# A router that counts instead of searching, four-byte token rows in 32 products, and an expert loop written out

## The reference, cut to what matters

```python
def moe_swiglu(h, router, w_in, w_out):
    b, s, d = h.shape
    t = h.reshape(b * s, d)
    logits = (t @ router).astype(jnp.float32)
    top_vals, top_idx = lax.top_k(logits, TOP_K)
    gates = jax.nn.softmax(top_vals, axis=-1)
    combine = jnp.sum(jax.nn.one_hot(top_idx, N_EXPERTS, dtype=jnp.float32) * gates[..., None], axis=1)
    y = jnp.zeros_like(t)
    for e in range(N_EXPERTS):
        y = y + combine[:, e:e + 1].astype(t.dtype) * swiglu(t, w_in[e], w_out[e])
    return y.reshape(b, s, d)
```

## Time and profile before

| | us |
|---|---|
| median of 3 runs (1569.7 to 1570.82) | 1569.99 |
| the profiled execution, its device time | 1570.96 |
| its span, first to last instruction | 1569.2 |
| around the span | 1.76 |
| PE busy | 1513.6 (96%) |
| DVE busy | 1199.7 (76%) |
| ACT busy | 994.5 (63%) |
| mean granted clock of PE | 0.986 |

### The profile page before, as it was taken

How to read it: one execution, slowest core, us unless ns; L and a number is a source line. 1 busy time by engine, 2 the same in 40 slices (tenths; PEclk the granted TensorE clock), 3 DMA queues, 4 the chain that set the end, 5 groups by cost and what they waited for, 6 DMA issues and landing times.

```text
span 1569.2 us, 21897 instructions
## 1 busy us (share of the span) xinstructions
PE 1513.6 (96%) x8223; PEld 1276.2 (81%) x8223; DVE 1199.7 (76%) x1033; ACT 994.5 (63%) x855; POOL 127.1 (8%) x192
## 2 busy tenths in 40 slices
PE   6999999999999699999999999999998999999998
PEld 6967999989997478888888877888887888888886
DVE  6966544565485768888888888888987888888887
ACT  5657433465545567776776676677776677677774
POOL 8900000000152300000000000000000000000000
PEclk9979999999999899999999999999999999999999
DMA  9503655546500369999999999999998999999994
GB/s 302 188 1 120 210 183 186 186 149 200 184 32 21 127 242 368 336 366 341 348 360 345 348 340 335 355 346 360 354 341 323 340 347 364 347 343 366 346 364 163
DMA packets 205346, 426.88 MB, mean 272 GB/s; under 512 B 6737, under 2 KB 56074, under 8 KB 205242
## 3 DMA queue, kind: packets, MB, share of 16 engines
q1 hardware_dynamic: 204880, 424.78, 76.6%
q0 software_dynamic: 320, 0.69, 0.2%
q10 hardware_dynamic: 42, 0.01, 0.0%
HBM read 424.41 MB, written 1.05 MB: 271 GB/s over the span
## 4 chain that ended last, share of the span: by engine, by line
PE 68%; DVE 2%; ACT 1%; issue 1%; DVEq 0%; ACTq 0%
PE bank L1287 20%; PE bank L1288 20%; PE bank L1289 20%; PE bank L1541 2%; PE bank L1647 2%; PE bank L1618 1%; DVE w_l L275 1%; PE bank L1523 0%; PE bank L1522 0%; PE bank L1631 0%; PE bank L1630 0%; ACT w_h L270 0%; PE bank L1554 0%; DVE h_l L511 0%; PE bank L1564 0%
## 5 line engine op out<-in xcount | busy, mean ns | idle before, releaser
L275 DVE TENSOR_TENSOR w_l<-raw,w_h 128x2048 fp32r<-128x2048 f32 x403 | 922.0, 2291 | 259.1 <-ACT w_h L270 258.1
L270 ACT ACTIVATE w_h<-raw 128x2048 fp32r<-128x2048 f32 x403 | 772.8, 1918 | 404.3 <-PE bank L1289 402.3
L1287 PE MATMUL bank<-w_h,hs_h 128*128 128x512 f32 x896 | 359.5, 401 | 6.5 <-issue 2.6
L1288 PE MATMUL bank<-w_l,hs_h 128*128 128x512 f32 x896 | 353.5, 395 | 3.7 <-issue 3.7
L1289 PE MATMUL bank<-w_h,hs_l 128*128 128x512 f32 x896 | 353.8, 395 | 0.0
L1287 PEld LDWEIGHTS bank<-w_h,hs_h 128*128 128x128 f32 x896 | 168.1, 188 | 45.2 <-issue 3.0
L1289 PEld LDWEIGHTS bank<-w_h,hs_l 128*128 128x128 f32 x896 | 168.0, 187 | 44.9 <-issue 4.1
L1287 PE MATMUL bank<-h_h,w_h 128*128 128x256 f32 x672 | 193.0, 287 | 6.3 <-DVE h_l L511 6.3
L1288 PEld LDWEIGHTS bank<-w_l,hs_h 128*128 128x128 f32 x896 | 168.3, 188 | 37.9
L1288 PE MATMUL bank<-h_l,w_h 128*128 128x256 f32 x672 | 191.1, 284 | 0.0
L1289 PE MATMUL bank<-h_h,w_l 128*128 128x256 f32 x672 | 191.0, 284 | 0.0
(11 more groups left out here) (275 smaller groups left out, 1413.0 us busy)
## 6 DMA issues: line engine op xcount, KB each, us to landing
raw<-in_moe_w_in SPq DMA_DIRECT2D x224, 1024.0 KB, 5.7
raw<-in_moe_w_out SPq DMA_DIRECT2D x112, 1024.0 KB, 5.5
raw<-in_ffn_w_in SPq DMA_DIRECT2D x22, 1024.0 KB, 5.1
raw<-in_hgrn_w_in SPq DMA_DIRECT2D x16, 1024.0 KB, 5.5
raw<-in_ffn_w_out SPq DMA_DIRECT2D x11, 1024.0 KB, 4.9
raw<-in_ab_w_in SPq DMA_DIRECT2D x10, 1024.0 KB, 11.7
raw<-in_ab_w_out SPq DMA_DIRECT2D x4, 1024.0 KB, 5.0
raw<-in_hgrn_w_out SPq DMA_DIRECT2D x4, 1024.0 KB, 4.9
```

Of the source, the lines that this page charges most:

```text
L270: act.activation(w_h[:, u0 % S, :], raw[:, u0 % R, :], ACT.Copy).then_inc(w_high, 1)
L275: eng.tensor_tensor(w_l[:, u0 % S, :], raw[:, u0 % R, :], w_h[:, u0 % S, :], ALU.subtract).then_inc(w_low, 1)
L1287: pe.matmul(o, a_high, b_high, start=start, stop=False, skip_group_check=True)
L1288: pe.matmul(o, a_high, b_low, start=False, stop=False, skip_group_check=True)
```

## The change

1. **Router by counting.** DVE compares each logit with the other seven of its token in one instruction of 128 elements (`above`, greater), once more with "greater or equal", takes the second where the other expert comes earlier (`earlier`), and adds up: a count of 0 is the first choice, of 1 the second, under 1.5 means chosen. The marks go to `chosen` in bf16 with zeros around, so that the ranks are two bf16 products and the expert totals a third. The gates (`gates`) are made after the first gather's results are out, and ACT's Exp moves behind `gather_high`. `slot_no` counts from 1, so that `rank` needs no -1.
2. **Token rows.** DVE makes `x_g` straight from `x` (`token_rows`, two instructions between those of the norm), ACT copies `x_h` (four bytes, F32R), DVE subtracts for `x_l` (`token_low`). POOL does none of it. A gather is 32 matmuls with `x_h`, `x_l` and a four-byte `sel`; `turn_selection` uses a four-byte identity.
3. **Order.** The lows of units `U_MOE + 1` and `U_MOE + 2` (`split_low`) move from ahead of the router to behind `choose` and behind `gather_low`.
4. **PE between.** Eight matmuls of 512 bf16 columns behind the turn of the logits, and three behind the ranks (`keep_warm`), whose results nothing reads.
5. **Experts.** In round 0 `moe_experts` writes all eight experts out, with no hardware loop.
6. **POOL's tables.** `span` and `lmask` share memory with layer 0's tensors, so POOL builds them after `o_part` 1, in the last unit of layer 0's attention output.

The diff, cut to these (the allocation, the semaphores' names and the round that isn't taken are left out):

```diff
+            if r == 0:
+                for e in range(NE):
+                    expert(e, e, 0, e % 2, e == NE - 1)
+                return
...
+            pool.wait_ge(o_part, 1)
             step(pool.memset(span[:].bitcast(F32), 1.0))
             step(pool.memset(lmask[:], 0))
...
-            for tt in range(TT):
-                pool.wait_ge(n_xn, 2 * (TT * 3 + tt) + 2)
-                pool.tensor_tensor(x_g[:, tt, :], xn[:, tt, :], gain_row[:], ALU.mult).then_inc(x_gain, 1)
-            for part in range(2):
-                for tt in range(TT):
-                    pool.wait_ge(x_part, 2 * part + tt + 1)
-                    dst = x_g[:, tt, :] if part == 0 else x_b[:, 2, tt, :]
-                    pool.tensor_tensor(dst, x_g[:, tt, :], x_b[:, part, tt, :], ALU.subtract).then_inc(x_gain, 1)
...
+            def token_rows(tt):
+
+                dve.wait_ge(gain_in, 16)
+                dve.scalar_tensor_tensor(out=x_g[:, tt, :], in0=x[:, tt, :], scalar=n_stat[:, 3, 4, tt:tt + 1], in1=gain_row[:],
+                                         op0=ALU.mult, op1=ALU.mult).then_inc(x_gain, 1)
+
+            def token_low(tt):
+
+                dve.wait_ge(x_high, tt + 1)
+                dve.tensor_tensor(x_l[:, tt, :], x_g[:, tt, :], x_h[:, tt, :], ALU.subtract).then_inc(x_low, 1)
...
             norm_low(3, C_FFN + 8)
-            split_low(dve, U_MOE + 1)
-            split_low(dve, U_MOE + 2)
+            token_low(0)
...
             dve.tensor_copy(logit_t[:], bank[0:NE, 4, 0:T]).then_inc(r_lc, 1)
+            token_low(1)
             dve.wait_ge(r_lg, 1)
             step(dve.tensor_copy(logit[:, 0, :, :], bank[:, 5, 0:TT * NE].rearrange("p (a e) -> p a e", a=TT)))
+            mine = logit[:, 0, :, :].unsqueeze(3).to_broadcast([P, TT, NE, NE])
+            other = logit[:, 0, :, :].unsqueeze(2).to_broadcast([P, TT, NE, NE])
+            dve.tensor_tensor(above[:, 0, :, :, :], other, mine, ALU.is_gt).then_inc(r_d, 1)
+            done[0] += 1
+            step(dve.tensor_tensor(above[:, 1, :, :, :], other, mine, ALU.is_ge))
+            step(dve.copy_predicated(above[:, 0, :, :, :], earlier[:], above[:, 1, :, :, :]))
+            step(dve.tensor_reduce(logit[:, 1, :, :], above[:, 0, :, :, :], AX.X, ALU.add))
+            dve.wait_ge(r_pad, 1)
+            step(dve.tensor_scalar(chosen[:, 1:3, 0:NE], logit[:, 1, :, :], 1.5, None, ALU.is_lt))
+            n_const["sel"] = done[0]
...
                 choose(0, r, 0)
                 if r == 0:
-                    step(dve.tensor_reduce(pick[:, 9, 0:1], bank[:, 4, TT * NE:(TT + 1) * NE], AX.X, ALU.max))
+                    split_low(dve, u + 1)
+                    dve.wait_ge(r_rank, 2)
...
                 gather_low(n0, 0)
+                if r == 0:
+                    split_low(dve, u + 2)
+                    gates()
...
+            for tt in range(TT):
+                act.wait_ge(x_gain, tt + 1)
+                act.activation(x_h[:, tt, :], x_g[:, tt, :], ACT.Copy).then_inc(x_high, 1)
+            act.wait_ge(const, n_const["early"])
+            act.activation(ident_r[:], ident[:], ACT.Copy).then_inc(id_r, 1)
             split_high(act, U_MOE + 2)
...
                 gather_high(n0, 0)
+                if r == 0:
+                    act.wait_ge(r_d, n_const["exp"])
+                    act.activation(pick[:, 5, :], pick[:, 4, :], ACT.Exp).then_inc(r_e, 1)
+                    table(ACT.Silu)
                 split_high(act, u + 3)
...
+            keep_warm(8, 7)
             pe.wait_ge(r_d, n_const["sel"])
-            s0, s1 = logit[:, 6, 0, :], logit[:, 6, 1, :]
-            pe.matmul(bank[:, 4, 0:NE], before[:], s0, start=True, stop=True)
-            pe.matmul(bank[:, 4, NE:2 * NE], ones[:], s0, start=True, stop=False)
-            pe.matmul(bank[:, 4, NE:2 * NE], before[:], s1, start=False, stop=True)
-            pe.matmul(bank[:, 4, 2 * NE:3 * NE], ones[:], s0, start=True, stop=False)
-            pe.matmul(bank[:, 4, 2 * NE:3 * NE], ones[:], s1, start=False, stop=True).then_inc(r_rank, 1)
+            pe.matmul(bank[:, 4, 0:P], before_b[:], chosen[:, 1:3, :], start=True, stop=False)
+            pe.matmul(bank[:, 4, 0:P], ones_b[:], chosen[:, 0:2, :], start=False, stop=True).then_inc(r_rank, 1)
+            pe.matmul(bank[:, 3, 0:P], ones_b[:], chosen[:, 1:3, :], start=True, stop=True).then_inc(r_rank, 1)
+            pe.wait_ge(id_r, 1)
+            keep_warm(3, 7)
...
-                            for part in range(3):
-                                last = pe.matmul(bank[:, 5 + i, c * P:(c + 1) * P], x_b[:, part, tt, f], sel[:, b, tt, :],
+                            for part, rows in enumerate((x_h, x_l)):
+                                last = pe.matmul(bank[:, 5 + i, c * P:(c + 1) * P], rows[:, tt, f], sel[:, b, tt, :],
...
-                    last = pe.matmul(bank[:, 7, tt * P:(tt + 1) * P], sel[:, b, tt, :], ident_h[:], start=True, stop=True)
+                    last = pe.matmul(bank[:, 7, tt * P:(tt + 1) * P], sel[:, b, tt, :], ident_r[:], start=True, stop=True)
```

More of the change, by code:

```diff
@@ L94, in build @@
         ident = sb("ident", [P, P])
-        ones = sb("ones", [P, P])
         mean_all = sb("mean_all", [P, P])
         mean_64 = sb("mean_64", [P, P])
-        before = sb("before", [P, P])
+        before_b = sb("before_b", [P, P], BF16)
+        ones_b = sb("ones_b", [P, P], BF16)
+        earlier = sb("earlier", [P, TT, NE, NE], I8)
+        ident_r = sb("ident_r", [P, P], F32R)
         slot_no = sb("slot_no", [P, 2, P])
@@ L308, in _ @@
                 pool.dma_start(router[:], A["moe_router"][0].rearrange("(c p) e -> p c e", p=P)).then_inc(rout_in, 16)
-            step(pool.memset(ones[:], 1.0))
+            step(pool.memset(ones_b[:], 1.0))
             step(pool.memset(mean_all[:], 1.0 / P))
@@ L830, in _ @@
-            step(dve.tensor_tensor(logit[:, 7, :, :], logit[:, 4, :, :], wide(pick[:, 7, :]), ALU.mult))
-            step(dve.tensor_tensor(logit[:, 8, :, :], logit[:, 5, :, :], wide(pick[:, 8, :]), ALU.mult))
-            step(dve.memset(comb[:], 0.0))
-            step(dve.memset(rank[:], -1.0))
-            step(dve.tensor_tensor(comb[:].rearrange("p (a e) -> p a e", a=TT)[:, :, 0:NE], logit[:, 7, :, :], logit[:, 8, :, :], ALU.add))
-            dve.wait_ge(r_rank, 1)
-            step(dve.scalar_tensor_tensor(out=logit[:, 9, :, :], in0=bank[:, 4, 0:TT * NE].rearrange("p (a e) -> p a e", a=TT), scalar=1.0,
-                                          in1=logit[:, 6, :, :], op0=ALU.add, op1=ALU.mult))
@@ L839, in _ @@
-            step(dve.tensor_scalar(rank[:].rearrange("p (a e) -> p a e", a=TT)[:, :, 0:NE], logit[:, 9, :, :], -1.0, None, ALU.add))
+            mine = logit[:, 0, :, :].unsqueeze(3).to_broadcast([P, TT, NE, NE])
[3 more added lines that the diff above has]
+            step(dve.tensor_tensor(above[:, 1, :, :, :], other, mine, ALU.is_ge))
@@ new lines, in _ @@
+            step(dve.tensor_reduce(pick[:, 0, :], logit[:, 0, :, :], AX.X, ALU.max))
+            step(dve.scalar_tensor_tensor(out=logit[:, 3, :, :], in0=logit[:, 4, :, :], scalar=-3.0e38, in1=logit[:, 0, :, :],
+                                          op0=ALU.mult, op1=ALU.add))
+            dve.wait_ge(r_rank, 1)
+            step(dve.scalar_tensor_tensor(out=rank[:].rearrange("p (a e) -> p a e", a=TT)[:, :, 0:NE],
+                                          in0=bank[:, 4, 0:P].rearrange("p (a e) -> p a e", a=TT)[:, :, 0:NE], scalar=1.0,
+                                          in1=chosen[:, 1:3, 0:NE], op0=ALU.add, op1=ALU.mult))
@@ L1199, in _ @@
             norm_high(3, C_FFN + 8)
-            split_high(act, U_MOE + 2)
-            for part in range(2):
-                for tt in range(TT):
-                    act.wait_ge(x_gain, 2 * part + tt + 1)
-                    act.activation(x_b[:, part, tt, :], x_g[:, tt, :], ACT.Copy).then_inc(x_part, 1)
-            act.wait_ge(r_d, n_const["exp"])
-            act.activation(pick[:, 5, :], pick[:, 4, :], ACT.Exp).then_inc(r_e, 1)
+            for tt in range(TT):
[3 more added lines that the diff above has]
+            act.activation(ident_r[:], ident[:], ACT.Copy).then_inc(id_r, 1)
+            split_high(act, U_MOE + 2)
+            table(ACT.Exp)
             def gather_high(n, b):
@@ L1260, in moe_round @@
                 n0, s0 = r * NE, r * NE * MOE_STEPS
-                act.activation(m_silu[:, 0:1], eps[:], ACT.Silu)
                 if r:
+                    act.activation(m_silu[:, 0:1], eps[:], ACT.Silu)
                     for i in range(3):
```

76 lines of the change are left out of this document (40 added, 36 removed).

## The result

| | before | after |
|---|---|---|
| median of 4 runs each, us | 1570.4 (1569.7 to 1572.36) | **1559.02** (1558.87 to 1561.73) |
| the profiled execution | 1570.96 | 1558.97 |
| its span | 1569.2 | 1556.9 |
| mean granted clock of PE | 0.986 | 0.992 |

The ratio is 0.993, with an interval of 0.9912 to 0.9947: 11.4 us less, where 13.5 less was forecast. The forecast of 1556.5 is 2.5 too low.

The account below looks back on a forecast made before the run. PE, busy for 96% of the span, was taken as the bound. Router -12.2, loop -9.6, gathers and turns +8.0, POOL +0.3 gave -13.5 us: 1557.4 profiled, 1556.5 as median, range 1551 to 1562.

Parts of the forecast that it names:

- Step 1: Router to first expert product: moved lows, no waits on POOL, fewer steps and an earlier first gather save 12.2 us.
- The clock: PE in router and first gather: fillers keep it at 2.4 GHz; the lower level would cost some 3.5 us more.
- What moved out: Lows of two units and ACT's Exp, moved behind the router, still come in time: 0, at most 1 us.
- Step 2: Experts' loop: writing it out removes all four PE gaps at its returns, 9.6 us less.
- Step 3: Seven other gathers on PE: 32 four-byte matmuls take 3.68 us each against 2.69, +6.9 us over seven.
- p: Price of one new four-byte gather matmul of 128 columns, set by its weight load: 0.115 us; break-even 0.165.
- Step 4: Turning the selection on PE: two matmuls of 0.045 us become two four-byte ones, eight times, +1.1 us.
- Step 5: POOL's tables, now built beside the norm behind layer 0's attention, slow DVE there: +0.3 us, ends 0 and 2.

Follow-up runs that it names:

- router_alone: Changed kernel with the experts' hardware loop back and the token rows as three bf16 parts with 48 products a gather; 1566.89 us, ratio 0.9976.
- unroll_only: Kernel before the change with only all eight experts written out in round 0; 1561.16 us, ratio 0.9933.
- split_64: Changed kernel with each gather product cut into two of 64 columns, 64 a gather, output not the reference's; 1623.55 us, ratio 1.0328.
- pad_32: Changed kernel with 32 bytes of nothing allocated ahead of `sel`, moving it and everything behind it; 1555.75 us, ratio 0.9898.
- no_fill: Changed kernel without the two groups of filling matmuls in the router, eight and three; 1564.06 us, ratio 0.995.

## Why the prediction was right, step by step

**Step 1, the router and the first gather (-12.2): right.** 12.69 less from the first filler to the first expert product. `x_g` cost 1.19 us a half by its distances and hid in the waits as assumed, the eight fillers ended at 531.5 ahead of the mark, and the predicted copy took 0.30. The gather's own clock held. By itself, in *router_alone*, this part brought 3.7 us of the whole, as told there.

**The clock: right for the gather, and a term missing behind it.** I asked whether the clock would hold up to the gather and not what the 1.7 us of waiting behind it would do. It fell at 539.1 for 3.4 us and stretched some eight products by 0.2 each; putting fillers there removed it, 1.5 us by the rows.

**What moved out, at 0: right.** PE waits for no `w_l` there; DVE has the low of `U_MOE + 2` done at 541.0 (542.9 counted from the same start as the kernel before), ahead of the 543.5 that I reckoned with.

**Step 2, the loop (-9.6): right.** *unroll_only* gives 9.56 by its rows. The reading that each return has its two gaps was a reading of one program, though: in the changed program the loop costs 5.6.

**Step 3, the gathers (+6.9): right in mechanism, mis-sized.** p is 0.110 and not 0.115: seven times 0.84, +5.9. *split_64* shows that the columns don't set it, which leaves the load as the likeliest. Step 4 came out as 0.13 a turn, +1.0.

**Step 5, POOL's tables (+0.3): about right.** These are four of POOL's selections and DVE's scalings in layer 0's norm, in the changed kernel:

```profile
139.73 2.88 POOL L303 TENSOR_SCALAR_AFFINE_SELECT span<-span 128x64 fp32r<-128x64 f32 x4
```

```profile
141.48 1.41 DVE L492 TENSOR_SCALAR xn<-x,n_stat 128x512 f32<-128x512 f32 x2
...
144.79 1.06 DVE L492 TENSOR_SCALAR xn<-x,n_stat 128x512 f32<-128x512 f32 x2
```

Without POOL beside them such a pair takes 0.88 (519.61 in the same trace, and both pairs in the kernel before): 0.7 us lost, 0.53 in one pair and 0.18 in the other, where one selection takes 0.72. The rule of the Trainium skill ("SBUF — State Buffer", section "Who interferes with whom"), by which the two exclude each other, fits these sizes; the price was 0.7 and not up to 4, and no run isolates it.

**Missing, the products' distance.** An expert takes 126.70 us, and 125.29 in *unroll_only* (634.03 to 1385.77 for six). Of the 1.41 between, 0.84 is the gather and 0.13 the turn; the other 0.44, eight times 3.5 us, is the distance. It is the largest error, and it came with the allocation, which I never read as part of the change. And one thing helped that is luck and no part of the change: the clock's low stretches in the first 110 us fall a little differently from one execution to the next. The profiled one of the changed kernel stands 1.9 us ahead at the norm's fillers (519.58 for 521.51); in *pad_32*, which does the same work up to there, they start at 521.29. *no_fill*, also the same up to there, had the clock's low stretches of the kernel before (6.8 us from about 15 and 17.1 from about 84) and started them at 522.05, half a microsecond later than the kernel before; that agrees with a small loss by POOL's tables. So some 2.5 us of the profiled run's gain are luck, and they hide part of the two missing terms; one of the four runs took 1561.73, just inside the range of 1551 to 1562.

The sum as measured, on the profiled runs: -1.9 (start, with POOL's 0.7 in it) - 12.7 - 9.6 + 5.9 + 1.0 + 1.5 + 3.5 = -12.3, and the spans differ by 12.3.

## What to carry to other kernels

Fewer products are not less work when each is short: up to 128 columns a four-byte product with its own load costs 0.110 us, where a whole bf16 pair takes 0.056, so 48 bf16 products beat 32 four-byte ones. A loop body whose return leaves TensorE idle with nothing in the data to wait for is worth writing out once. When a change touches the allocation, compare the distance of the untouched matmuls in both traces before explaining anything else by it; and look for idle time behind a filled stretch as well as before it.

## What the hardware showed that I had not expected

- The place of the expert operands modulo 256 bytes shifts the distance of a 512-column four-byte product from 233.0 to 234.2 ns (all fourteen kernels follow it), 3.8 us over six experts. The Trainium skill ("SBUF — State Buffer", section "Who interferes with whom") says that TensorE waits on no other engine's access; no run here shows whether this is such a wait, only that the place counts.
- A loop's return cost PE one gap of 2.5 us in one program, and a second one of 0.7 to 1.9 us some 5.6 us later in others. The same gap let the clock fall in *router_alone* and not in the kernel before.
- 64 products of 64 columns in a row, at 0.11 each, let the clock fall within every gather, also where PE had not idled ahead of it; 32 of 128 columns at the same 0.11 never did. They last half as long, so which of the two counts isn't shown.
- At the low clock the four-byte product of 128 columns costs twice as much too: 0.214 in *no_fill*'s first gather for 0.110 at the full clock.
